# Gate and up products of the feed-forward by Strassen's block products, in a two-block transformer kernel on one core

## The reference

```
h2 = rmsnorm(x, gain)
x  = x + (silu(h2 @ w_gate) * (h2 @ w_up)) @ w_down     # 1024 x 2816, 1024 x 2816, 2816 x 1024
```

## Time and profile before

| | us |
|---|---|
| median of 3 runs | 3095.77 (3095.16 to 3097.09) |
| span of the profiled execution, first to last instruction | 3092.8 |
| PE busy | 3032.8 |
| DVE busy | 1683.1 |
| ACT busy | 1205.3 |
| POOL busy | 288.2 |
| gate and up stages, four | tiles at 10.88 each in the steady part |

### The profile page before, as it was taken

The page is one execution under the profiler, slowest core; times in us unless marked ns, Lnnn a source line. Parts: engine busy times, 40 slices in busy tenths (PEclk is TensorE's granted clock), DMA queues, the critical chain, the costliest instruction groups (busy, mean ns, idle before and its releaser), DMA issues.

```text
span 3092.8 us, 40119 instructions
## 1 busy us (share of the span) xinstructions
PE 3032.8 (98%) x15272; PEld 2463.6 (80%) x15272; DVE 1683.1 (54%) x3050; ACT 1205.3 (39%) x2238; POOL 288.2 (9%) x344
## 2 busy tenths in 40 slices
PE   8999999999999999999999999999999999999998
PEld 7888887788888888778678888888778768888887
DVE  6653364446565426656756555436556766555434
ACT  4322334443432224644543322224545553322223
POOL 0000110001100012011001000013111001100002
PEclk9999999999999999999999999999999999999999
DMA  5333373225233233225125223334224315322332
GB/s 172 111 96 114 109 148 125 92 88 178 92 102 100 93 108 110 81 100 163 69 73 173 96 96 97 95 110 142 91 91 132 116 39 182 104 96 96 99 99 96
DMA packets 105999, 338.18 MB, mean 109 GB/s; under 512 B 15360, under 2 KB 15888, under 8 KB 105680
## 3 DMA queue, kind: packets, MB, share of 16 engines
q1 hardware_dynamic: 84816, 272.45, 27.4%
q0 software_dynamic: 20992, 63.15, 6.8%
HBM read 299.24 MB, written 27.52 MB: 106 GB/s over the span
## 4 chain that ended last, share of the span: by engine, by line
PE 90%; ACT 3%; DVE 3%; issue 2%; DMA 1%; POOL 0%; SPq 0%; POOLq 0%; DVEq 0%; ACTq 0%
PE bk L1655 26%; PE bk L1657 26%; PE bk L1656 26%; PE bk L1731 3%; PE bk L1753 2%; PE bk L1739 2%; ACT t L1893 1%; PE bk L1694 1%; PE bk L1695 1%; PE bk L1696 1%; DVE t L1974 1%; ACT t L1901 1%; ACT t L1841 0%; DVE t L2124 0%; PE bk L1707 0%
## 5 line engine op out<-in xcount | busy, mean ns | idle before, releaser
L1655 PE MATMUL bk<-t,t 128*128 128x512 f32 x3784 | 1483.5, 392 | 20.4 <-DVE t L1974 12.5
L1657 PE MATMUL bk<-t,t 128*128 128x512 f32 x3784 | 1469.7, 388 | 0.0
L1656 PE MATMUL bk<-t,t 128*128 128x512 f32 x3784 | 1468.1, 388 | 0.0
L1655 PEld LDWEIGHTS bk<-t,t 128*128 128x128 f32 x3784 | 712.8, 188 | 170.1 <-issue 19.7
L1657 PEld LDWEIGHTS bk<-t,t 128*128 128x128 f32 x3784 | 712.5, 188 | 147.0
L1656 PEld LDWEIGHTS bk<-t,t 128*128 128x128 f32 x3784 | 713.4, 189 | 141.6
L1974 DVE TENSOR_TENSOR t<-t,t 128x1024 fp32r<-128x1024 f32 (+3 forms) x538 | 615.6, 1163 | 370.2 <-ACT t L1841 369.7
L1841 ACT CAST t<-t 128x1024 fp32r<-128x1024 f32 (+3 forms) x538 | 513.6, 983 | 221.9 <-PE bk L1657 118.7
L1884 ACT CAST t<-t 128x512 fp32r<-128x512 f32 x88 | 54.7, 622 | 433.5 <-DVE t L2034 433.5
L1893 ACT ACTIVATE t<-t,t 128x256 f32<-128x256 f32 (+3 forms) x336 | 173.9, 519 | 123.0 <-DVE t L2047 122.4
L2280 POOL TENSOR_TENSOR t<-t,t 128x512 f32<-128x512 f32 x58 | 78.3, 1350 | 1387.0 <-ACT t L1871 1387.0
(11 more groups left out here) (173 smaller groups left out, 2008.7 us busy)
## 6 DMA issues: line engine op xcount, KB each, us to landing
t<-in_f_g SPq DMA_DIRECT2D x88, 512.0 KB, 4.3
t<-in_f_u SPq DMA_DIRECT2D x88, 512.0 KB, 3.5
t<-in_f_d SPq DMA_DIRECT2D x64, 512.0 KB, 4.4
t<-in_gate SPq DMA_DIRECT2D x48, 512.0 KB, 3.6
gate_scratch<-t POOLq DMA_DIRECT2D x64, 256.0 KB, 2.3
t<-gate_scratch POOLq DMA_DIRECT2D x64, 256.0 KB, 3.9
t<-in_f_d SPq DMA_DIRECT2D x32, 384.0 KB, 3.1
t<-in_wo SPq DMA_DIRECT2D x24, 512.0 KB, 3.7
```

What stands on the lines that cost most here:

```text
L1655: pe.matmul(o, wh, xh, start=start, stop=False)
L1656: pe.matmul(o, wh, xl, start=False, stop=False)
L1657: return pe.matmul(o, wl, xh, start=False, stop=stop)
```

## The change

In each feed-forward tiles 0 and 1 stay as they are (`plain=2`; `f2` has `wide=1` now). Tiles 2 to 21 are made by `pair`. With the features in halves (chunks 0 to 3 and 4 to 7), the tokens in halves (0 to 255 and 256 to 511) and the output in gate and up, the work of one tile is a 2x2 by 2x2 block product; Strassen's scheme takes 7 block products in place of 8. Each is 4 chunks x 3 matmuls of 256 columns, so 84 matmuls of 256 columns for a tile in place of 48 of 512.

For this the weights need sums and differences of their 128x512 blocks: POOL makes four (`total`, products 5, 6, 3, 7), ACT makes seven casts of 128x512 (`cast`), DVE seven rests of 128x512 (`rest`). The activation's sums and differences (`forms` 4 to 7) are made once for each feed-forward: ACT lifts `xT` times gain, POOL subtracts in place (16 subtractions of 128x256, `lift`), ACT and DVE split them (16 each of 128x256). Two of the forms lie where `xT` lies, so `xT` is first stored to HBM (`park`, 8 DMAs on POOL; `f1` has it there already) and loaded again behind the stage (8 DMAs on POOL). The products' sums are partly in PSUM and partly made behind: ACT copies four 128x256 results out (`snap`), DVE adds (`gate_low`, `gate_high`, `ups`). `ups` adds one PSUM result to both halves of the up tile; the up half is scaled by `rstd` behind that on DVE (`scale`), and the product of gate and up goes to POOL (`product`).

In the class `Plan`, the loop of `ffn` (`made` and `lifts` order the lifting within the two plain tiles):

```diff
+        lifts = iter([lambda: (lift(0), lift(1), form(0)), lambda: (lift(2), form(1)), lambda: (lift(3), form(2)),
+                      lambda: form(3)])
...
-        for j in range(j0, FC):
-            two = self.dense([(name + "_g", j, 0, list(range(8)))], self.hs(ht)) + self.dense(
-                [(name + "_u", j, 0, list(range(8)))], self.hs(ht))
+        for j in range(j0, plain):
+            two = self.dense([(name + "_g", j, 0, list(range(8)))], self.hs(ht))
+            next(lifts, lambda: None)()
+            two += self.dense([(name + "_u", j, 0, list(range(8)))], self.hs(ht))
+            next(lifts, lambda: None)()
...
-            gate_up(works, free + self.rope_done if hook is not None and j == 13 else free)
+            if j < plain - 1:
+                gate_up(works, free)
             if hook is not None:
                 next(hook, None)
...
+        us = [self.pair(name, j, (FC - 1 - j) % 2 ^ 1, slots, homes, None) for j in range(plain, FC)]
+        self.step("pair_in", U=us[0], load_to=us[0]["u"] + 1)
+        gate_up(works, free)
...
+            U["x"] = {1: ht[0:4], 2: ht[4:8], 3: ht[4:8], 4: made, 5: made, 6: made, 7: made}
+            self.step("pair", U=U, V=us[v + 1] if v + 1 < len(us) else None, Z=us[v - 1] if v else None, load_to=U["u"] + 2)
+            if v:
+                emptied(us[v - 1])
+            if hook is not None and v % 4 != 3:
+                next(hook, None)
...
-        xs = self.ffn("f2", ht, wide=2)
+        xs, xt = self.ffn("f2", ht, xt, 4, xt, self.D["park"], wide=1)
```

On PE (`U` is this tile, `V` the next one, `Z` the one before), the products in the order 1, 5, 2, 6, 4, 3, 7, each by:

```diff
+    def product(U, k, o, opens, lo, x):
+        u = U["u"]
+        e.wait_ge(("h", k, u), ("l", k, u), *U["x"][k])
+        for c in range(4):
+            wh = P.ph[k][:, c * 128:(c + 1) * 128]
...
+            xh, xl = x(c)
+            pe.matmul(o, wh, xh, start=opens and c == 0, stop=False, skip_group_check=True)
+            pe.matmul(o, wh, xl, start=False, stop=False, skip_group_check=True)
+            ins = pe.matmul(o, wl, xh, start=False, stop=c == 3, skip_group_check=True)
```

On ACT:

```diff
+            U, V, Z = s["U"], s["V"], s["Z"]
+            if Z:
+                cast(U, 3)
+                bend(Z)
+            snap(U, 1)
+            if Z:
+                cast(U, 7)
+            snap(U, 5)
+            if V:
+                cast(V, 1)
+            if Z and V:
+                hidden(Z)
+            if V:
+                cast(V, 2)
+            snap(U, 6)
+            if V:
+                cast(V, 5)
+            snap(U, 4)
+            if V:
+                cast(V, 4)
+                cast(V, 6)
```

On DVE, where each `rest` is one subtraction of 128x512 with both inputs in SBUF:

```diff
+    def ups(U):
+        u = U["u"]
+        e.wait_ge(("P", 7, u), ("m", 4, u), ("m", 5, u))
+        u2 = U["uu"][:].rearrange("p (a b) -> p a b", a=2)
+        vec(dve.tensor_tensor(u2, U["bank"][0].unsqueeze(1).broadcast_to([128, 2, 256]), u2, ALU.add), ("c2", u))
+
+    def scale(U):
+        u = U["u"]
+        e.wait_ge(("c2", u), U["r"])
+        vec(dve.tensor_tensor(U["uu"][:], U["uu"][:], P.rstd[:], ALU.mult), ("ur", u))
...
+            if Z:
+                rest(U, 2)
+                ups(Z)
+                rest(U, 6)
+                rest(U, 3)
+                scale(Z)
+                bent(Z)
+                rest(U, 7)
+            if V:
+                rest(V, 1)
+            gate_low(U)
+            if Z and V:
+                hidden(Z)
+            if V:
+                rest(V, 5)
+                rest(V, 4)
+                e.parted = V["u"] + 1
+            gate_high(U)
```

On POOL, where each `total` is one 128x512 addition or subtraction with both inputs in SBUF:

```diff
+    def product(U):
+        u = U["u"]
+        e.wait_ge(("z", u), ("ur", u))
+        e.then_inc(pool.tensor_tensor(U["g"][:], U["g"][:], U["uu"][:], ALU.mult), "pools", ("prod", u))
...
+            if Z:
+                total(U, 7)
+                product(Z)
+            if V:
+                total(V, 5)
+                total(V, 6)
+                total(V, 3)
```

More of the change, by code:

```diff
@@ L179, in __init__ @@
         self.split_to = -1
+        self.ring, self.next_spl, self.next_raw = NSPL, 0, 0
+        self.raw_free = [[] for _ in range(NRAW)]
+        self.spl_free = [[] for _ in range(NSPL)]
         self.gate_at = {}
@@ L286, in abreast @@
         n = self.step("abreast", banks=[g[1] for g in got], bts=[g[2] for g in got], us=us, order=order,
-                      xs=[xs(c) for c in range(KC)], load_to=us[-1][0] + 4, split_to=us[-1][0] + 2)
+                      xs=[xs(c) for c in range(KC)], load_to=us[-1][0] + 4, split_to=us[-1][0] + ahead)
         self.stage()
@@ L470, in postnorm, with lift, formed, pair @@
         return new, ht
-    def ffn(self, name, ht, hook=None, wide=0):
+    def lift(self, i, gi, xt):
+        got = [self.tmp.take() for _ in range(2)]
+        n = self.step("lift", c=(i, i + 4), gi=gi, xt=[xt[i], xt[i + 4]], h=[g[1] for g in got], f=[g[2] for g in got])
+        def formed(free):
+            k = self.step("forms", i=i, h=[g[1] for g in got], t=(n, "p"), free=free)
+            for g in got:
+                self.tmp.give(g[0], (k, "a"), (k, "d"))
+            return (k, "d")
+        return formed
+    def pair(self, name, j, w, free, homes, stamp):
+        u = len(self.units)
+        wu, wg = self.pw[w]
+        U = dict(pair=True, u=u, j=j, w=w, wu=wu, wg=wg, free=dict(free), src=[self.D[name + "_u"][j], self.D[name + "_g"][j]],
+                 sem=[f"w{2 * w}", f"w{2 * w + 1}"], home=[homes[w, 0], homes[w, 1]])
+        self.units.append(U)
+        self.at["rawu", u] = [(f"w{2 * w}", self.fetched(f"w{2 * w}"))]
+        self.at["rawg", u] = [(f"w{2 * w + 1}", self.fetched(f"w{2 * w + 1}"))]
+        homes[w, 0], homes[w, 1] = [("P", 4, u), ("S", 7, u)], [("P", 2, u), ("S", 7, u)]
+        for k in range(1, 8):
+            free[k] = [("P", k, u)]
+        return U
+    def ffn(self, name, ht, xt, gi, busy, kept, hook=None, wide=0, plain=2):
         free = self.now()
-        hid = self.tile([128, 2, FC, T], self.RA, F32R)
+        hid = self.tile([128, FC, 2, T], self.RA, F32R)
         toks = {}
+        hidden = lambda j: (hid[:, j, 0, :], hid[:, j, 1, :])
+        n = 2 * plain
+        self.ring = 3
+        self.next_spl = self.next_raw = (2 - (n - 1)) % 3
+        t1_free = [self.spl_free[3], free]
         def gate_up(works, free):
@@ new lines, in ffn @@
+        for v, U in enumerate(us):
+            j = U["j"]
+            got = [(R, R.take()) for R in (self.PB, self.OB, self.PB, self.OB)]
+            U.update(banks=[(R, g[0]) for R, g in got], bank=[g[1][:, 0:256] for R, g in got], bts=[g[2] for R, g in got])
+            tm = [self.tmp.take() for _ in range(3)]
+            U.update(tmps=[g[0] for g in tm], g=tm[0][1], uu=tm[1][1], t=tm[2][1], tf=[g[2] for g in tm], r=self.rf_tok)
+            U["hi"], U["lo"] = hidden(j)
+            U["hid_free"] = [free, self.rope_done if hook is not None and 14 <= j <= 18 else None,
+                             ("P", 4, last) if j >= 20 else None]
+            U["x"] = {1: ht[0:4], 2: ht[4:8], 3: ht[4:8], 4: made, 5: made, 6: made, 7: made}
[4 more added lines that the diff above has]
+                next(hook, None)
@@ new lines, in ffn @@
+        if hook is not None:
+            assert next(hook, None) is None
+        self.raw_free = [homes[0, 0], homes[0, 1], homes[1, 0]]
+        self.spl_free = [[("P", 5, last), homes[1, 1]], [("P", 6, last)], [("P", 7, last)], [("P", 5, last)]]
+        self.Sr.free[3] = [self.Sr.free[3], ("P", 1, last)]
+        self.ring, self.next_spl, self.next_raw = NSPL, 3, 0
+        self.stream(2)
+        self.step("pair_out", Z=us[-1])
+        emptied(us[-1])
+        src = [self.D["xT"][:, c, :] if kept is None else kept[c] for c in range(KC)]
@@ L509, in attend @@
+        xt = [self.load(self.xT[:, c, :], src[c], ("P", 6 + c // 4, last)) for c in range(KC)]
+        return (lambda c: (*hidden(c), toks[c])), xt
     def attend(self, slots, fill=()):
@@ L1970, in rests @@
             u = e.parted
-            n = P.units[u][3]
+            U = P.units[u]
+            if U["pair"]:
+                break
             e.wait_ge(("hi", u))
-            hi, lo = (P.spl[u % NSPL][:, p, 0:n] for p in range(2))
-            e.then_inc(dve.tensor_tensor(lo, P.raw[u % NRAW][:, 0:n], hi.bitcast(F32), ALU.subtract), "rests", ("lo", u))
+            hi, lo = (U["spl"][:, p, :] for p in range(2))
+            e.then_inc(dve.tensor_tensor(lo, U["raw"], hi.bitcast(F32), ALU.subtract), "rests", ("lo", u))
@@ L2341, in build @@
     P = Plan(nc, D, out)
-    for u in range(len(P.units)):
-        P.at["raw", u] = [(f"w{u % NRAW}", 16 * (u // NRAW + 1))]
     with ExitStack() as ctx:
```

263 lines of the change are left out of this document (233 added, 30 removed).

## The result

The changed kernel takes **3420.31 us** (median of 4 runs, 3418.66 to 3422.58) against 3096.14 before on the same chip: 1.105 times as long (95% interval 1.1032 to 1.1064). The forecast was 3288, its range ended at 3375. The direction was right; the time is 132 us above the forecast and 45 above the range.

What follows compares the result with a forecast made beforehand. PE was taken to bound the stage before, VectorE and GpSimd taking turns at SBUF the changed tile. Terms 133 + 14 + 5.6 + 23 + 17 = 192.6, added to 3092.8 and 3.0 around it, gave 3288 us; range 3200 to 3375.

Steps and rivals of the forecast that it cites:

- The tile: Steady pair tile: VectorE and GpSimd take turns at SBUF, 12.85 us (12.05 to 13.4); +133 over four stages; chance 0.77.
- the chain product, hidden high, hidden low and the wait for product 3 leave some 0.2: In a pair tile: this chain, across engines, leaves some 0.2 us uncovered, part of the 12.85.
- The first two still run at PE's 10.1: First two of a stage's twenty pair tiles: nothing of a tile before them, so PE's 10.1 us each.
- Into and out of the pairs: Start and end of each pair stage: 1.5 us in and 2 out, four times 3.5, +14 (0 to 36).
- `f2` side by side: Start of `f2`: two units instead of four use the arriving chunks of `hT`, so PE waits; +5.6 us (4 to 7).
- Product 5 waits for all forms. That is just in time or a little late: 1.5: Entry to the pairs, behind the plain tiles: product 5 waits for the forms, 1.5 us (0 to 6) a stage.
- The hole in `f1`: Behind plain tile 1: sums queue behind table DMAs on GpSimd; PE stands 21 us, lower clock 2 more; +23 (15 to 27).
- The tables on VectorE: `f1` pair loop: 31 table-making instructions, 21 us in sum, lengthen it on VectorE; +17 us (8 to 22).
- Side by side: Rival, pair tiles: VectorE and GpSimd overlap, a tile is PE's 10.1 us; 3077 us, faster; chance 0.07.
- The lower clock in the tiles: Rival, pair tiles: PE's stands bring the lower clock, a tile takes 18.1 us; 3734 us; chance 0.03.
- Nothing overlaps at all: Rival, pair tiles: VectorE and GpSimd turns without the 0.15 us at each change, tile 14.5; 3410 us; chance 0.10.
- VectorE always wins the turn: Rival, pair tiles: GpSimd gets in only where VectorE waits; time stays in the range; no chance of its own.

Runs made afterwards that it cites:

- the kernel with the late hidden part: The changed kernel, all five GpSimd instructions kept, with VectorE's hidden-low instruction moved behind the next tile's two rests: 3448.04 us.

## Why the prediction was right in direction and short in size

The mechanism held: GpSimd was idle in this stage before, so its window could not show the meeting, and the three places where the two engines met told what would happen. The sum of 192.6 us should have been 325.5 (3418.3 less 3092.8). The stages below are compared matmul by matmul with those of the kernel before. By the steps of the prediction:

- **The tile, 12.85 forecast, 13.65 measured: the largest error, on 18 tiles a stage 58 us of 132.** Read from end to end in the rows above, the tile is eleven VectorE instructions at 0.60, 0.60 for the up half's addition, 0.53 for `gate_high`'s, and 5.92 for GpSimd's five turns. The step "the chain product, hidden high, hidden low and the wait for product 3 leave some 0.2" took `gate_high`'s PSUM addition as covered. It was not; covering it gave 0.52 a tile. And the turns were put at 5 x 1.09 = 5.45 by "A GpSimd instruction put between two of VectorE's". That is right for the sum for product 7, which cost 1.05; but product, sum 5, sum 6 and sum 3 follow one another with only the hidden low part between them, and then VectorE has nothing it may do beside them. Ends of GpSimd instructions came 1.15 to 1.36 behind the end ahead of them, and VectorE stood idle 2.8 us.
- **"The first two still run at PE's 10.1".** Only the second did. From product 1 to the next tile's product 1 the third block's first tile takes 14.0, with PE at the lower clock behind the gap ahead of it and 1.8 us of waiting for product 6, and its second tile 10.2. With what is at the last tile this is 4.5 us a stage, some 18. From the first product to the end of the last the stage took 269.7 for 217.6 before, +52.1, where +33.2 was forecast; four times it is 208 for 133.
- **Into and out of the pairs (14) and `f2` side by side (5.6): 19.6 forecast, some 72 measured** (what the other points leave of the 325.5). The way out was right: 1.6 a stage where 2 was forecast. The step "Product 5 waits for all forms. That is just in time or a little late: 1.5" failed. Between its first matmul and product 1 the third stage lost 14.9 us, and the fourth as much: PE waited at the first swiglu and then for product 1, not 5. I had counted GpSimd's own time and not the order on ScalarE and VectorE behind it: the copy of rstd and the first swiglu stand behind casts and forms, and product 1's rest behind the last forms. The whole third and fourth stage are 68.8 and 68.5 longer. `f2` is 74.5 longer, with a gap of 9.0 in its head, and PE comes to it 3.7 later still. Moving that work changed where PE waits more than how long; fewer things in the block's head were not tried.
- **The hole in `f1`, 23 forecast, 29.5 measured**: its first two tiles take 53.8 us from product 1 to product 1, where the third block's take 24.2. PE's start-to-start gaps of 20.6 and 5.9 stand in them, with the lower clock behind each. The chain is as described, 45.53 to 63.28 on GpSimd, and starting it early gave back 16.5.
- **The tables on VectorE, 17 forecast, 16.3 measured**: eight tiles of 14.4 to 16.6 us in `f1` where those instructions stand.
- **The rivals.** Side by side (3077) is out: the same sums on VectorE are 168 us faster, though VectorE has more to do. The lower clock in the tiles (3734) is out: 1.00 over the stage. Nothing overlaps at all gave 3410, near the result, but by a tile of 14.5 that was not there: the rows show a VectorE instruction ending 0.55 behind GpSimd's and not 0.69. Its figure is near by luck, because the entries, which it did not hold, made up the rest. The Trainium skill (SBUF — State Buffer, section Who interferes with whom) has the loser fully blocked; the rows agree but for that 0.15 us. VectorE always wins the turn was seen in part: the product waits until both of two rests are through, as at 2102.06.

What a GpSimd instruction costs in this tile, over the same work on VectorE: the product alone 0.88 us a tile (12.53 against 11.65), four sums 0.76 together (12.41), all five 2.00. They do not add up, since turns and in-order waits fall under one another. With all five on GpSimd the port is shown to be the cause: writes that read nothing, though shorter, give back 3.6 and bring the rests to 686 ns, the holding on the ring is 3.5, and moving VectorE's wait away loses 0.35. For the lone product the split of the 0.88 stays open: moving the wait gained 0.09, and in its place 0.77 was holding and 0.66 a wait for ScalarE, less the 0.60 that VectorE has no longer to do.

Why no version wins follows from three numbers. A Strassen tile is 10.05 us of PE and not 7/8 of 10.88, for 84 matmuls of 256 columns at 0.12 are dearer for their columns than 48 of 512 at 0.227 (at 2.4 GHz 0.89 columns a cycle against 0.94, where the text above has one); that leaves 0.83. VectorE with the sums needs 17 x 0.60 + 2 x 0.33 = 10.9, no less than the tile before. And an entry costs some 14 us even with four plain tiles and sums that read nothing, which 17 tiles of 0.83 would have to earn first.

## What to carry to other kernels

Before work is put on an idle engine, write one steady tile as a list of turns on the resource that both engines share, in order, and count what runs when the newcomer follows itself, not only when it stands between two others. Then do the same for the transition into the loop: a recurring entry cost of 14 us decides a change that can give 0.8 us a tile at best. A cheap first trial is to put the new work on the engine that already waits; if that is faster, the helper is not helping.

## What was not expected of the hardware

- **A short stand of PE, and the lower clock behind it.** In the kernel with the late hidden part PE stands once a tile, 2.47 to 2.90 us from start to start. In the third block 11 of 18 such stands were followed by some 16 matmuls 0.21 apart instead of 0.12, and 7 were not, among them the longest, of 2.90; the granted clock of the window shown is 0.86. So the length of the stand alone doesn't decide it, and what else does is open. It cost nothing there: the tile is 14.0 with it and without. In the changed kernel PE stands three times a tile, at most 1.95 but for one of 2.30 in the third block, and the clock is 1.00. PE's rows of the late one:

```profile
2142.09 0.28 PE L1789 MATMUL bk<-t,t 128*128 128x256 f32 x1
2144.59 0.39 PE L1787 MATMUL bk<-t,t 128*128 128x256 f32 x1 [2.21 <-DVE t L2221]
...
2145.23 0.41 PE L1788 MATMUL bk<-t,t 128*128 128x256 f32 x1
2145.45 0.41 PE L1789 MATMUL bk<-t,t 128*128 128x256 f32 x1
```

- **Who got the turn.** GpSimd's product, issued while a rest ran, let that rest and the next one pass (2102.06, 2030.53); when a rest had itself been held by GpSimd, the next GpSimd instruction came ahead of the next rest (the 3.51 at 2107.39 with the sum that began at 2108.61 and ended at 2110.35).
- **A write alone takes no turn.** GpSimd's writes of 128x512, 528 ns each, left VectorE's rests at 686.
